# Quarter blocks of 32, 8 and 2 in place of seven halving levels in a chunked GLA scan, with the gate logits split over two row halves

## The reference, cut to what matters

```python
log_a = jax.nn.log_sigmoid((lr @ w_gate_up + b_gate).astype(jnp.float32)) / GATE_TAU   # lr: rank 16
...
bcum = jnp.cumsum(ac, axis=1)
diff = bcum[:, :, None] - bcum[:, None, :]
decay = jnp.exp(jnp.where(causal[None, :, :, None, None], diff, -jnp.inf))
att = jnp.einsum('bijhd,bjhd->bhij', qc[:, :, None] * decay, kc)
o = (jnp.einsum('bhij,bjhe->bihe', att, vc)
     + jnp.einsum('bihd,bhde->bihe', qc * jnp.exp(bcum), S))
```

## Time and profile before

| | before |
|---|---|
| median of three runs | 1818.34 us (1818.22 to 1819.02) |
| the profiled execution | 1818.22 us, of which the instructions span 1816.4 us |
| TensorE busy | 1785.9 us, 98% |
| VectorE, ScalarE, GpSimd busy | 748.9, 509.3, 513.1 us |
| TensorE's mean granted clock | 0.994 |

### The profile page before, as it was taken

How to read it: one execution, slowest core, us unless ns; L and a number is a source line. 1 busy time by engine, 2 the same in 40 slices (tenths; PEclk the granted TensorE clock), 3 DMA queues, 4 the chain that set the end, 5 groups by cost and what they waited for, 6 DMA issues and landing times.

```text
span 1816.4 us, 30442 instructions
## 1 busy us (share of the span) xinstructions
PE 1785.9 (98%) x11013; PEld 1663.2 (92%) x11013; DVE 748.9 (41%) x1517; ACT 509.3 (28%) x1205; POOL 513.1 (28%) x438
## 2 busy tenths in 40 slices
PE   6999999999999999999999999999999999999999
PEld 5999999989999999999999999999999888878887
DVE  7655540454434411111455554543221453453433
ACT  6311110134333410000344344430011343333332
POOL 4255430322232243342444444443324000000000
PEclk8999999999999999999999999999999999999999
DMA  7323211343444331221333432244443675664653
GB/s 258 134 79 86 80 51 38 97 110 101 111 112 118 92 110 54 80 71 53 110 85 93 116 98 84 84 126 148 143 123 113 209 253 163 206 221 163 197 168 133
DMA packets 245804, 221.10 MB, mean 122 GB/s; under 512 B 25857, under 2 KB 210337, under 8 KB 244274
## 3 DMA queue, kind: packets, MB, share of 16 engines
q1 hardware_dynamic: 171794, 177.07, 31.3%
q10 hardware_dynamic: 73944, 43.15, 8.7%
HBM read 170.03 MB, written 52.24 MB: 122 GB/s over the span
## 4 chain that ended last, share of the span: by engine, by line
PE 95%; DVE 2%; DMA 1%; ACT 1%; issue 0%; SPq 0%; POOL 0%; ACTq 0%; DVEq 0%
PE p L1717 20%; PE p L1719 19%; PE p L1718 19%; PE p L1808 7%; PE p L1810 7%; PE p L1812 7%; PE p L838 3%; PE p L581 1%; PE p L1752 1%; PE p L1751 1%; PE p L1753 1%; PE p L609 1%; PE p L593 1%; PE p L849 1%; PE p L856 1%; PE p L850 1%
## 5 line engine op out<-in xcount | busy, mean ns | idle before, releaser
L1717 PE MATMUL p<-x_hi,w_lo 128*128 128x384 f32 x2016 | 699.5, 347 | 0.0
L1719 PE MATMUL p<-x_hi,w_hi 128*128 128x384 f32 x2016 | 676.1, 335 | 0.0
L1718 PE MATMUL p<-x_lo,w_hi 128*128 128x384 f32 x2016 | 675.2, 335 | 0.0
L1717 PEld LDWEIGHTS p<-x_hi,w_lo 128*128 128x128 f32 x2016 | 379.8, 188 | 15.4 <-issue 13.3
L1718 PEld LDWEIGHTS p<-x_lo,w_hi 128*128 128x128 f32 x2016 | 380.0, 188 | 0.2
L1719 PEld LDWEIGHTS p<-x_hi,w_hi 128*128 128x128 f32 x2016 | 379.1, 188 | 0.0
L537 POOL TENSOR_TENSOR w_hi<-raw,small 128x512 fp32r<-128x512 f32 x164 | 174.2, 1062 | 724.5 <-PE p L1719 724.2
L541 POOL TENSOR_TENSOR w_lo<-raw,w_hi 128x512 fp32r<-128x512 f32 x164 | 215.1, 1312 | 12.9
L1997 DVE TENSOR_TENSOR w_lo<-raw,w_hi 128x512 fp32r<-128x512 f32 x192 | 132.2, 691 | 205.0 <-ACT w_hi L1665 205.0
L1665 ACT ACTIVATE w_hi<-raw 128x512 fp32r<-128x512 f32 x192 | 120.6, 631 | 240.5 <-PE p L1812 213.2
L1808 PE MATMUL p<-w_hi,x_lo 128*128 128x512 f32 x576 | 162.1, 390 | 1.1 <-DVE w_lo L1997 1.1
(11 more groups left out here) (174 smaller groups left out, 1753.7 us busy)
## 6 DMA issues: line engine op xcount, KB each, us to landing
raw<-in_w_out SPq DMA_DIRECT2D x192, 256.0 KB, 3.3
raw<-in_w_in SPq DMA_DIRECT2D x164, 256.0 KB, 4.5
h_t<-xn SPq DMA_DIRECT2D x126, 192.0 KB, 1.9
work<-h_t SPq DMA_DIRECT2D x24, 384.0 KB, 6.0
out<-work SPq DMA_DIRECT2D x36, 256.0 KB, 4.5
work<-h_t ACTq DMA_DIRECT2D x16, 512.0 KB, 5.3
work<-h_t ACTq DMA_DIRECT2D x32, 256.0 KB, 3.7
work<-in_x_prompt SPq DMA_DIRECT2D x32, 256.0 KB, 4.9
```

What stands on the lines that cost most here:

```text
L1717: pe.matmul(out, w_lo[:, k, :], x_hi[:, k, tok], start=(k == 0), stop=False)
L1718: pe.matmul(out, w_hi[:, k, :], x_lo[:, k, tok], start=False, stop=False)
L1719: mm = pe.matmul(out, w_hi[:, k, :], x_hi[:, k, tok], start=False, stop=(k == KT - 1))
```

## The change

The seven levels of halves become three levels of quarters (s = 32, 8, 2): a block of 4s tokens is cut into quarters, and each of the three earlier quarters is paired with all the later ones, 6 quarters of 4 in all, so 192 columns a head. The level of s = 1 is folded into the diagonal's matmul: beside the 128 columns of q come 64 columns of the odd tokens' q times their own decay (`l_odd`), 192 columns a head. Logits of two heads go to partitions 0 to 16 and those of the other two to 64 to 80, each half with its own bank. Steps move: logits 6 to 4, turn 9 to 10 with a new wait for the log decay (since both now use bank ub[3]), keys 22 to 18, values 30 to 22, levels at 29, 33, 41. The last take moves ahead of the gating of groups 0 and 1. On GpSimd and VectorE a level has four instructions for one or two, and a take has six.

```diff
-LEVELS = (64, 32, 16, 8, 4, 2, 1)
-DEC_LEVELS = (8, 4, 2, 1)
+LEVELS = (32, 8, 2)
+DEC_LEVELS = LEVELS[1:]
+SAME = 3 * P // 2
+PAIRS = 6 * P // 4
...
             def logits():
-                pe.wait_ge(sl_lr, 16 * t + 16)
+                pe.wait_ge(sl_lr, 32 * t + 32)
                 pe.wait_ge(sl_up, 4 * t + 1)
-                for h in range(N_GLA):
-                    mm = pe.matmul(ub[0][:, h * P:h * P + P], w_up_sb[:, h * P:h * P + P], lr[:, :],
-                                   start=True, stop=True)
+                for e in range(2):
+                    for half in range(2):
+                        rows = slice(half * HEAD_DIM, half * HEAD_DIM + RANK + 1)
+                        mm = pe.matmul(log_bank[half][:, e * P:e * P + P], w_up_sb[rows, e * P:e * P + P], lr[rows, :],
+                                       start=True, stop=True)
...
             def diagonal():
...
-                pe.wait_ge(sl_la, t + 1)
+                pe.wait_ge(sl_la, 2 * t + 2)
+                pe.wait_ge(sl_og, 4 * t + 1)
                 for h in range(N_GLA):
...
+                    mm = pe.matmul(same_bank[h // 2][:, (h % 2) * SAME:(h % 2) * SAME + SAME], l_k[:, h * P:h * P + P],
+                                   l_qo[:, h, :], start=True, stop=True)
...
+                    mm = pe.matmul(ub[at + h // 2][:, (h % 2) * PAIRS:(h % 2) * PAIRS + PAIRS],
+                                   l_k4[s][:, h * P:h * P + P], l_q4[s][:, h, :], start=True, stop=True)
...
             def turn(decoded=False):
                 if not decoded:
                     pe.wait_ge(sl_up, 4 * t + 5)
+                    pe.wait_ge(sl_la, 2 * t + 3)
...
-            stages = {6: logits, 14: diagonal, 22: keys, 30: values, 47: outputs}
+            stages = {4: logits, 14: diagonal, 18: keys, 22: values, 47: outputs}
             if not first:
-                stages[9] = linear_stages(pe, t - 1)[-1]
-            for i, step in enumerate((23, 25, 28, 32, 35, 38, 42)):
+                stages[10] = linear_stages(pe, t - 1)[-1]
+            for i, step in enumerate((29, 33, 41)):
...
             def load_lr(self, t):
-                self.act.dma_start(lr[0:RANK, :], h_t[LR0:LR0 + RANK, ds(t * P + PAD, P)]).then_inc(sl_lr, 16)
+                for half in range(2):
+                    self.act.dma_start(lr[half * HEAD_DIM:half * HEAD_DIM + RANK, :],
+                                       h_t[LR0:LR0 + RANK, ds(t * P + PAD, P)]).then_inc(sl_lr, 16)
...
+                act.wait_ge(sl_la, 2 * t + 1)
+                act.activation(l_odd, odd(four(l_e[1])), ACT.Exp, scale=1.0 / TAU).then_inc(sl_a, 1)
...
             def first(self):
                 dve = self.dve
                 dve.wait_ge(sb_w, 16 * 6)
+                dve.memset(far, 0.0)
...
+                for half in range(2):
+                    cols = slice(half * 256, half * 256 + 256)
+                    ins = dve.scalar_tensor_tensor(out=l_e[1][:, cols], in0=log_bank[half][:, 0:256], scalar=0.0,
+                                                   in1=l_e[0][:, cols], op0=ALU.min, op1=ALU.subtract)
+                ins.then_inc(sl_la, 1)
...
+                z, k = (blocks(x, s)[:, :, 0:3 * s] for x in (l_k4[s], l_k))
+                dve.tensor_tensor(z, k, z, ALU.mult)
+                for b in range(3):
+                    z = paired(l_q4[s], s, b)
+                    ins = dve.tensor_tensor(z, later(l_q, s, b), z, ALU.mult)
+                ins.then_inc(sl_zz, 1)
...
-            stages = {3: logits, 6: linear_stages(self.pe, T - 1)[-1], 12: diagonal, 18: keys, 32: values}
-            for i, step in enumerate((20, 22, 25, 28)):
+            stages = {2: logits, 10: linear_stages(self.pe, T - 1)[-1], 14: diagonal, 18: keys, 39: values}
+            for i, step in enumerate((30, 35)):
...
-            pool.tensor_copy(tables_sb[:, :], work[:, 2 * D_MODEL:2 * D_MODEL + M_ALL]).then_inc(s_tables, 1)
+            for c in range(0, M_ALL, M_PIECE):
+                cols = slice(c, min(c + M_PIECE, M_ALL))
+                pool.tensor_copy(tables_sb[:, cols], work[:, 2 * D_MODEL + c:2 * D_MODEL + cols.stop])\
+                    .then_inc(s_tables, 1)
...
-            item(J_ATT, norm_before=True, stages=attend_pe(pe, 0, first=True))
+            item(J_ATT, norm_before=True, stages=attend_pe(pe, 0, first=True), sum_at=4)
```

More of the change, by code:

```diff
@@ L773, in four @@
             return x.rearrange("p (h n) -> p h n", h=N_GLA)
[L775 to L785, removed]
+        l_qo = four(work[:, 0:N_GLA * SAME])
+        l_q, l_odd = l_qo[:, :, 0:P], l_qo[:, :, P:SAME]
+        l_k = work[:, 768:1280]
+        l_v = work[:, 1280:2304]
+        l_vtok = work[:, 2304:3328]
+        l_b = work[:, 3328:3840]
+        l_e = [work[:, 3840:4352], work[:, 4352:4864]]
+        l_z = work[:, 4864:5376]
+        l_att = work[:, 5376:5888]
+        l_qe = work[:, 5888:6400]
+        l_ktok = work[:, 6400:6912]
+        l_s = work[:, 6912:7936]
+        l_og = work[:, 7936:8960]
         l_o = l_v
@@ L789, in project, with blocks, later, odd @@
         NZ = 2 + len(LEVELS)
-        def halves(x, s):
-            return x.rearrange("p (n two s) -> p n two s", two=2, s=s)
+        far = work[:, 8704:9216]
+        l_k4 = dict(zip(LEVELS, (far, l_e[0], far)))
+        l_q4 = dict(zip(LEVELS, (four(work[:, at:at + N_GLA * PAIRS]) for at in (7936, 4352, 7936))))
+        same_bank = (ub[0], ub[4])
+        log_bank = (ub[0], ub[3])
+        def blocks(x, s):
+            return x.rearrange("p (m n) -> p m n", n=4 * s)
+        def later(x, s, b):
+            return x.rearrange("p h (m n) -> p h m n", n=4 * s)[:, :, :, (b + 1) * s:4 * s]
+        def odd(x):
+            return x.rearrange("p h (m two) -> p h m two", two=2)[:, :, :, 1]
+        def paired(x, s, b):
+            n = (3 - b) * s
+            return x[:, :, QUAD_AT[b]:QUAD_AT[b] + (3 - b) * P // 4].rearrange("p h (m n) -> p h m n", n=n)
+        HALVES = 2 + 4 * len(LEVELS)
+        def two(x):
+            return x.rearrange("p (h n) -> p h n", h=2)
+        def two_heads(x, h):
+            return two(x[:, 2 * P * h:2 * P * h + 2 * P])
+        def quad_bank(s):
+            return 1 if s == LEVELS[1] else 3
         def linear_stages(pe, t, dec=False):
@@ L981, in part_0 @@
                     self.decays(t)
+                    self.keys(t)
                     self.level(t, 0, LEVELS[0])
-                    self.keys(t)
-                    for i in range(1, 4):
-                        self.level(t, i, LEVELS[i])
+                    self.values(t)
                 def part_1():
-                    self.values(t)
-                    for i in range(4, 7):
+                    for i in range(1, len(LEVELS)):
                         self.level(t, i, LEVELS[i])
@@ L2064, in shape_constants @@
     m = np.zeros((P, M_ALL), np.float32)
+    m[:, 0:M_QUAD] = np.tile(np.arange(P)[:, None] == 2 * np.arange(P // 2), (1, 2))
     for i, s in enumerate(LEVELS):
-        n = P // (2 * s)
-        pairs = np.kron(np.eye(n), np.concatenate([np.ones((s, s)), np.zeros((s, s))]))
-        m[:, i * 256:i * 256 + 256] = np.tile(pairs, (1, N_GLA))
-    m[:, M_DIAG:M_SCAN] = np.tile(np.eye(P), (1, N_GLA))
+        keys = np.concatenate([np.repeat(4 * np.arange(P // (4 * s)) + b, (3 - b) * s) for b in range(3)])
+        at = M_QUAD + i * 2 * PAIRS
+        m[:, at:at + 2 * PAIRS] = np.tile(np.arange(P)[:, None] // s == keys, (1, 2))
+    m[:, M_DIAG:M_SCAN] = np.tile(np.eye(P), (1, 2))
     m[:, M_SCAN:M_SCAN_DEC] = np.arange(4 * P) % P > 0
```

184 lines of the change are left out of this document (112 added, 72 removed).

## The result

| | before | after |
|---|---|---|
| median | 1818.22 us (1815.15 to 1819.02, 7 runs) | 1824.08 us (1820.08 to 1828.11, 7 runs) |
| the profiled execution | 1818.22 us, span 1816.4 us | 1828.11 us, span 1826.3 us |
| item period, logits of one GLA tile to the next, tiles 1 to 6 | 40.82 us | 41.5 to 43.5 us |

The ratio is 1.0036, 95% interval 1.0023 to 1.0049: slower by 0.4%, a small change but clear of the noise. Executions of the kernel after differ by 8 us among themselves, and the profiled one is the slowest of the seven. The forecast was 1812.1 us with a range of 1800 to 1822. The sign was wrong and the time lies outside the range.

What follows compares the result with a forecast made beforehand. The prediction took TensorE's queue to bound the GLA items. From 1818.2 us it added 0.1 for the GLA items (savings cancelled by waits), -5.2 and -1.0 for two early places: 1812.1 us, range 1800 to 1822.

Steps and rivals of the forecast that it cites:

- the term that decides: Values' stage of GLA tiles: values land 17.4 us into the item, wanted at 15.5, so TensorE waits 1.9 us (0.4 to 3.5).
- TensorE's work: GLA items: levels, diagonal and logits together save 2.41 us a prompt tile, 1.02 us in the decode tile, 20.3 us in all.
- The values' load: ScalarE's queue in GLA tiles: issued about 10.0 us into the item, landing 7.3 us later on average (6.4 to 8.8).
- The clock: TensorE's clock in GLA items: expected to stay at full speed behind the values' waits, costing nothing in the sum.
- rival 1: GLA items: clock falls behind values' waits, up to 2.8 us each, about 1824 us; chance 0.18 shared with two others.
- Tile 0: First GLA tile: waits of 1.9 and 1.3 us, net 2.4 us, using up all of its saving.
- The decode item: Last GLA item: 1.02 us less work; its turn waits 1.2 us against 0.7 us of waits today, 0.5 us more.
- The chain of levels: GpSimd, ScalarE and VectorE work for GLA levels: 0.7 to 1.1 us of slack, so costed at nothing.
- The masked copies: Takes' copies in GLA tiles: 0.44 us each alone, zero cost; at 0.75 us, outputs would wait about 1.5 us a tile.
- The two early places: The wait at 70 us with the clock behind it, -5.2 us, and J_ATT's sum ahead of the scores, -1.0 us.
- Rival 3: GLA tiles: values come in time, seven tiles give 1 to 1.5 us each, 1802 to 1806 us; chance 0.22.
- Rival 4: GLA stages: row halves don't run side by side, or 192-column passes take 0.216 us; 1822 us, chance 0.18 shared with others.

Runs made afterwards that it cites:

- experiment 6: The changed kernel with SyncE issuing the next item's four weight loads only once the tile's values have landed, not for the last tile: 1807.32 us, ratio 0.9943.
- experiment 2: The changed kernel with the values' load issued before the outputs' store instead of behind it, values at step 22: 1833.96 us, ratio 1.0093.
- Experiment 1: The changed kernel with the values' transposes at step 27 instead of 22: 1820.53 us, ratio to before 1.0018.
- experiment 3: The kernel before with only the cast in pieces of 512 and J_ATT's sum of squares ahead of its first scores: 1812.42 us, ratio 0.9974.
- experiment 10: Experiment 6 with the last tile's weights held too, later steps in tile 0 and decode item, turn at 11, values at 23: 1805.36 us, ratio 0.9928.
- experiment 8: Experiment 6 with all four gate logit products in the first row half; one profiled execution, logits stage as long as before the change, no kernel time given.
- experiment 5: Experiment 1 with levels at 31, 35, 43, and tile 0's logits, diagonal, keys and far-key clearing later: 1830.63 us, ratio 1.007.

## Why the prediction was wrong

**What bounds the kernel**, read from the waits and the timeline, was right: TensorE's queue, and behind the change the landings.

**The step that failed** is the one that the prediction itself called the term that decides: values there at S + 17.4, so a wait of 1.9 us a tile, with the clock at full speed behind it. Both parts were too small, the wait by the duration of the load and the clock by being put at nothing in the sum.

**TensorE's work** was right to 0.1 us. Levels, diagonal and logits cost 1.30, 1.30 and 0.84 us. The turn lost 0.57 us a tile (0.36 of it as a wait in the list), 0.6 forecast. -2.41 + 0.57 = -1.84 us a tile without the values' wait; experiment 6 has it: 39.01 - 40.82 = -1.81 us.

**The values' load** was issued at S + 10.0 as forecast. The first failed term is its duration: I took 7.3 us, the mean of before's own loads, and a range around it. It took 8.0 by the median, and the seven waits came to 17.2 us instead of 7 x 1.9 = 13.3: +3.9 us. From start to start each cost 0.22 us more than the list has (the stage takes 3.72 us with a wait of 2.62 in it, and 0.88 without), another 1.5 us. The reason was in the prediction's own sentence, and I didn't follow it. Store, values and four weight loads share the engines. Here are the store and the first weight load of one tile, before and after:
```profile
997.21 0.41 ACTq L971 DMA_DIRECT2D o_t<-work  x1
...
997.90 3.86 SPq L371 DMA_DIRECT2D raw<-in_w_in  x4
```
```profile
997.89 3.19 SPq L380 DMA_DIRECT2D raw<-in_w_in  x4
...
998.37 0.47 ACTq L1035 DMA_DIRECT2D o_t<-work  x1
```
Before, the store goes ahead of the first weight load in all seven tiles and the load in six of them. Moved 1.0 to 1.1 us, the store is issued behind it, and the load behind two or three of them. A mean of old durations doesn't hold for a transfer that is moved past another queue's. Experiments 2 and 6 show that the durations follow the company: 4.6 us first, 5.0 without the weights, 8.0 behind them. That the order makes the step from 7.3 to 8.0 is read from these issue times and not tested alone; that the weights make the load late as a whole is what experiment 6 shows.

**The clock** is the second failed term. I had it as rival 1, with the right place, a price of the same order for a fall (up to 2.8 us forecast) and the right total, 1824 us, and gave it, together with two others, 0.18. The evidence that I set against it was one wait of 1.8 us without a fall. With seven or eight waits of 1.9 us and more, lying between a case with and one without a fall, a chance for each wait was wanted, not one for all. Less its listed wait, a tile took 40.8 us with a fall in it and 39.2 us without, so each of the three cost 1.6 us, 4.7 us together.

**Tile 0** lost 1.9 us ahead of its logits, as forecast, and then the clock for 6.7 us: the same step failed there. In experiment 6 the same 1.92 us wait passed without a fall, the diagonal then waited 1.2 us, and the item took 40.95 us. Here, with the clock down, the diagonal didn't wait, and the item took 42.6 us: the fall cost 1.7 us and not half of 6.7.

**The sum.** It can be drawn up for the profiled execution alone, from the starts of the items' first products: 1828.1 us against 1812.1, 16.0 us too much. Tiles 1 to 7 took 297.0 us where 7 x 40.9 = 286.3 were forecast, 10.7 us more: 5.4 us by the waits, 4.7 us by the clock. Tile 0 took 42.6 us where 40.8 was forecast, 1.8 us more. The decode item took 34.3 us where 33.1 was forecast, 1.2 us more: its turn, its keys and its first level waited 1.0, 0.4 and 0.3 us. The part ahead of the GLA items gave 5.0 us instead of 6.2. Behind the input projection's items the kernel took 1.0 us more than before, which the sum had at nothing. There is no profile of the other six executions, so how the median's 12.0 us divide is not shown; that their clocks fell a different number of times would fit the spread of 8 us, and is not shown either.

**The chain of levels** "costed at nothing" was right in the list of waits (L893 waited 0.6 us in all) and wrong in its reason. It had no slack of its own: the late values covered it. I let GpSimd begin when it was free, and didn't write down what its first level waits for, the landing of the outputs' store. The view that tells it is GpSimd's group of L1207 after the change:
```profile
L1207 POOL TENSOR_TENSOR work<-work 128x384 f32<-128x384 f32 x26 | 22.0, 847 | 83.7 <-DMA o_t<-work 42.3 <-PE p L893 34.2 <-PE p L876 7.2
```
42.3 us of idling behind that store. Experiment 1 uncovered it (1.25 + 0.4 us a tile), and experiment 2 made it the bound.

**The masked copies** took 0.39, 0.29 and 0.25 us by their width on average, near what I took, and the outputs never waited for them.

**The two early places** came nearly as forecast: -5.2 and -1.0 us in the prediction, and -5.6 us measured for both in experiment 3. There item 1 takes 27.45 instead of 32.35 us (-4.9), while J_ATT and the item behind it give only 0.3 us together.

**Rival 3** (values in time) gave 1802 to 1806 us; experiments 6 and 10 ended near it, at 1807.3 and 1805.4 us, once they were in time. **Rival 4** fell: a pass of 192 columns takes 0.162 us, and experiment 8 shows the halves side by side.

**Still open**: why the clock falls behind one wait of 2.42 us and not behind another of 2.65; the decode item's 0.85 us at its first level, which didn't move with the step; and the 1.0 us at the kernel's end, which stands in every profiled kernel with the change (398.8 to 399.8 us behind the items, against 397.3 to 398.0 without it).

## What to carry to other kernels

When a step is moved earlier or a DMA issue later, look at which transfers of other queues it passes, and price the transfer by that company, not by its mean. Write beside each stage all that it waits for, buffers' releases by stores included: when the wait that ends last goes, the one behind it takes over, here with 1.2 of 2.5 us. And a transfer that nobody needs soon, like weights read 20 us later, should be held behind those that TensorE is about to need; here two lines gave 17 us.

## What the runs showed of the hardware

- Four weight loads issued on one queue raise a store on the other queue from 3.5 to 5.5 us and a load from 5.0 to 8.0 us.
- TensorE's granted clock fell from 1.00 to 0.50 behind waits of 1.92 to 3.5 us, but not behind each: three of seven values' waits after the change, four of eight of about 2.0 us in experiment 5. One and the same wait of 1.92 us ahead of tile 0's logits was followed by a fall in experiment 8 and by none in experiment 6. Waits of 1.85 us and less were never followed by a fall in the profiles of this study, once the first 31 us were over.
- VectorE's multiplications of two SBUF operands take twice their time beside GpSimd's weight split (1.13 against 0.56 us for 384 elements), and 0.70 us beside its subtractions of 384 elements.
- Products of 17 rows in the two row halves of the array start in pairs even when they are issued one half after the other.
